# Three double slots in every gate/up chunk but the first, and each double slot's own remainder ahead of its weight sums

## What is computed

```python
D_MODEL, SEQ, D_FF = 2048, 256, 5632

def swiglu(h, wg, wu, wd):
    return (jax.nn.silu(h @ wg) * (h @ wu)) @ wd
...
x = x + 0.5 * swiglu(rmsnorm(x, ffn1_norm[i]), ffn1_wg[i], ffn1_wu[i], ffn1_wd[i])
x = x + hybrid_mixer(rmsnorm(x, mix_norm[i]), ...)
x = x + 0.5 * swiglu(rmsnorm(x, ffn2_norm[i]), ffn2_wg[i], ffn2_wu[i], ffn2_wd[i])
```

## Time and profile before

| | |
|---|---|
| median of 3 runs | 1819.16 us (1819.10 to 1820.21) |
| the profiled execution | 1821.51 us, its span 1819.7 us |
| TensorE matmuls busy | 1806.8 us, 99%, 8151 instructions |
| TensorE weight loads busy | 1486.1 us, 82% |
| VectorE busy | 1529.6 us, 84% |
| ScalarE busy | 1021.6 us, 56% |
| GpSimd busy | 247.9 us, 14% |
| granted TensorE clock | 0.999 of full speed, mean |
| DMA | 367.12 MB, mean 202 GB/s |

### The profile page before, as it was taken

One profiled execution on the slowest core, in us unless ns is written; L12 is line 12 of the kernel. 1 busy time (PEld: TensorE's weight loads), 2 busy tenths in 40 slices (PEclk: granted clock), 3 DMA queues, 4 the chain that ended last, 5 costly groups with the idle time before them and its releaser, 6 DMA issues.

```text
span 1819.7 us, 22566 instructions
## 1 busy us (share of the span) xinstructions
PE 1806.8 (99%) x8151; PEld 1486.1 (82%) x8152; DVE 1529.6 (84%) x1821; ACT 1021.6 (56%) x1320; POOL 247.9 (14%) x442
## 2 busy tenths in 40 slices
PE   9999999999999999999999999999999999999998
PEld 6888888888888888888788888888888888888886
DVE  7999898889888987678567867899888889988897
ACT  6555555455555555556577745555555455555554
POOL 2111111001111100000123300111111000221100
PEclk9999999999999999999999999999999999999999
DMA  7676766667767667766543655767767666777764
GB/s 242 210 218 205 218 205 216 194 200 211 227 199 216 199 212 211 207 207 199 151 131 113 208 174 184 215 204 218 213 196 211 218 203 191 218 216 213 234 210 149
DMA packets 199276, 367.12 MB, mean 202 GB/s; under 512 B 19012, under 2 KB 23856, under 8 KB 199056
## 3 DMA queue, kind: packets, MB, share of 16 engines
q1 hardware_dynamic: 185008, 352.37, 63.3%
q0 software_dynamic: 11648, 12.02, 2.2%
q10 hardware_dynamic: 2528, 1.52, 0.3%
HBM read 350.11 MB, written 4.19 MB: 195 GB/s over the span
## 4 chain that ended last, share of the span: by engine, by line
PE 75%; DVE 14%; DMA 7%; issue 2%; ACT 1%; DVEq 0%; ACTq 0%
PE ps L765 19%; PE ps L767 19%; PE ps L766 19%; DMA raw<-in_ffn_wu_dram 5%; PE ps L783 5%; PE ps L784 5%; PE ps L785 5%; DVE w_lo L1820 5%; DVE wt L1882 2%; PE ps L832 2%; DVE wt_lo L1892 1%; DVE wt L1885 1%; DMA raw<-in_ffn_wd_dram 1%; DVE wt L1887 1%; DVE w_lo L1900 1%
## 5 line engine op out<-in xcount | busy, mean ns | idle before, releaser
L1304 ACT ACTIVATE w_hi<-raw 128x1024 fp32r<-128x1024 f32 x579 | 609.4, 1059 | 415.3 <-PE ps L767 253.1
L1820 DVE TENSOR_TENSOR w_lo<-raw,w_hi 128x1024 fp32r<-128x1024 f32 x579 | 700.7, 1227 | 88.3 <-ACT w_hi L1304 84.4
L765 PE MATMUL ps<-w_hi,hT_hi 128*128 128x512 f32 x1356 | 531.3, 392 | 0.6 <-DVE w_lo L1820 0.4
L767 PE MATMUL ps<-w_hi,hT_lo 128*128 128x512 f32 x1356 | 528.3, 390 | 0.0
L766 PE MATMUL ps<-w_lo,hT_hi 128*128 128x512 f32 x1356 | 528.0, 389 | 0.0
L706 POOL DMA_DIRECT2D gu_raw<-gu_sq x352 | 187.8, 542 | 1082.1 <-DVE gu_sq L2057 1010.1
L765 PEld LDWEIGHTS ps<-w_hi,hT_hi 128*128 128x128 f32 x1356 | 254.7, 188 | 54.1 <-DVE w_lo L1820 2.5
L767 PEld LDWEIGHTS ps<-w_hi,hT_lo 128*128 128x128 f32 x1356 | 254.5, 188 | 53.7
L766 PEld LDWEIGHTS ps<-w_lo,hT_hi 128*128 128x128 f32 x1356 | 254.7, 188 | 51.3
L1355 ACT ACTIVATE wt_hi<-wt 128x1024 fp32r<-128x1024 f32 x152 | 160.3, 1055 | 164.1 <-DVE wt L1882 164.1
L765 PE MATMUL ps<-w_hi,guT_hi 128*128 128x512 f32 x496 | 193.0, 389 | 0.0
(11 more groups left out here) (306 smaller groups left out, 2156.2 us busy)
## 6 DMA issues: line engine op xcount, KB each, us to landing
raw<-in_ffn_wu_dram SPq DMA_DIRECT2D x176, 512.0 KB, 4.8
raw<-in_ffn_wd_dram SPq DMA_DIRECT2D x176, 512.0 KB, 4.9
raw<-in_ffn_wg_dram SPq DMA_DIRECT2D x175, 512.0 KB, 4.5
raw<-in_w_in_dram SPq DMA_DIRECT2D x88, 512.0 KB, 3.8
raw<-in_w_out_dram SPq DMA_DIRECT2D x32, 512.0 KB, 4.4
gu_raw<-gu_sq POOLq DMA_DIRECT2D x352, 32.0 KB, 3.7
x_parked<-x SPq DMA_DIRECT2D x8, 256.0 KB, 5.3
raw<-in_cmp_k_w_dram SPq DMA_DIRECT2D x8, 256.0 KB, 3.2
```

The lines of the kernel that those rows point to most:

```text
L765: mm(o, x_hi, w_hi[:, s, kk, :], start=begin, stop=False, skip_group_check=skip)
L767: ins = mm(o, x_lo, w_hi[:, s, kk, :], start=False, stop=last and kk == GK - 1, skip_group_check=skip)
L1304: act.activation(w_hi[:, c % SLOTS, :, :], raw[:, c % SLOTS, :, :], ACT.Copy).then_inc(hi_ready, 1)
L1820: tt(w_lo[:, s, :, :], raw[:, s, :, :], w_hi[:, s, :, :].bitcast(F32), ALU.subtract).then_inc(lo_ready, 1)
```

## The change

All gate/up chunks but the first take the table with three double slots, so 7 chunks of each FFN get one more (14 in all). The gate additions, the Silus and the sums for up of every chunk move to steps 0 and 1 of what follows. ScalarE's `gu_operand` and `gs_high` go to steps 9 and 11, VectorE's `gu_sums` to step 10 and its `gu_operand` to step 14 (9 in chunks 5, 6 and 10, which have no sums to make for the chunk before). In every double slot, those of the first chunk and of the down jobs too, VectorE makes the slot's own remainder first and the sums behind it. Since the sums now read a raw tile whose remainder is already done, SyncE waits for `t_ready` too before it loads such a buffer again. The core of the diff:

```diff
-CHUNK = [(GATE, 0), (GATE, 1), (GATE, 4), (GATE, 5), (GATE, 6), (PAIR, 2), (PAIR2, 2), (GATE, 7),
-         (UP, 0), (UP, 1), (PAIR, 3), (PAIR2, 3), (UP, 4), (UP, 5), (UP, 6), (UP, 7)]
...
+CHUNK = [(GATE, 0), (GATE, 4), (GATE, 5), (GATE, 6), (PAIR, 1), (PAIR2, 1), (GATE, 7), (UP, 0),
+         (PAIR, 2), (PAIR2, 2), (UP, 4), (UP, 5), (PAIR, 3), (PAIR2, 3), (UP, 6), (UP, 7)]
+NO_SUMS = (5, 6, 10)
...
-PAIRS = 2
+PAIRS = 3
...
-TURN_STEPS = [0, 1, 2, 3, 7]
+TURN_STEPS = [0, 1, 2, 3, 14]
...
                 if c >= SLOTS:
-                    sp.wait_ge(lo_ready, count(c - SLOTS + 1, i, per))
+                    sp.wait_ge(lo_ready, c - SLOTS + 1)
+                for f in range(2):
+                    if c - SLOTS - FFN0[f] in PAIR_SLOTS:
+                        sp.wait_ge(t_ready, pair_no(f, c - SLOTS) + 1)
...
                     for p, (kind, _) in enumerate(chunk_table(n)):
                         slot(f, c + p, kind, i)
-                        if n - 1 in LATE and n != PART0[1] and p < NT:
-                            late_silu(f, n - 1, p)
                         if n != PART0[1]:
-                            if p == gu_at:
+                            if p < NT:
+                                late_silu(f, n - 1, p, i)
+                            if p == 9:
                                 gu_operand(f, n - 1, i)
-                            if p == gu_at + 1:
+                            if p == 11:
                                 gs_high(n - 1, quad_no(f, n - 1), i)
...
-                        if p == 14 and n not in LATE:
-                            product1_copy(f, n, c + chunk_pairs(n)[-1], i)
-                        if p == 15 and n not in LATE:
-                            silu(f, n, i)
...
                     lo(c, i, CHUNK_SLOTS)
                     if kind == PAIR:
+                        weight_sums(f, c, i)
                         wt_low(f, c, 0, i)
-                if next_kind == PAIR:
-                    weight_sums(f, c + 1, i)
...
+                    low_at = 9 if n in NO_SUMS else 14
...
-                            if n - 1 in LATE and p == 0:
-                                gate_products(f, n - 1)
-                            if n - 1 in LATE and p == 1:
-                                right_sums(f, n - 1)
+                            if p == 0:
+                                gate_products(f, n - 1, i)
+                            if p == 1:
+                                right_sums(f, n - 1, i)
...
-                            if p == gu_at:
+                            if p == 10:
                                 gu_sums(f, n - 1, quad_no(f, n - 1), i)
-                            if p == gu_at + 1:
+                            if p == low_at:
                                 gu_operand(f, n - 1, quad_no(f, n - 1), i)
-                        if p == 14 and n not in LATE:
-                            gate_products(f, n, i)
-                            right_sums(f, n, i)
```

More of the change, by code:

```diff
@@ L596, in _, with load @@
         def _(sp):
-            def load(c, src, i=None, per=0, halves=None):
+            def load(c, src, halves=None):
                 if c >= SLOTS:
-                    sp.wait_ge(lo_ready, count(c - SLOTS + 1, i, per))
+                    sp.wait_ge(lo_ready, c - SLOTS + 1)
+                for f in range(2):
+                    if c - SLOTS - FFN0[f] in PAIR_SLOTS:
+                        sp.wait_ge(t_ready, pair_no(f, c - SLOTS) + 1)
                 s = c % SLOTS
@@ L1397, in silu, with late_silu @@
                                    scale=rs[:, RS_FFN2 if f else RS_FFN1, t:t + 1]).then_inc(silu_done, 1)
-            def late_silu(f, n, t):
+            def late_silu(f, n, t, i=None):
                 if t == 0:
-                    product1_copy(f, n, FFN0[f] + chunk_slot(n) + chunk_pairs(n)[-1])
-                silu(f, n, tiles=(t,))
+                    product1_copy(f, n, FFN0[f] + chunk_slot(n) + chunk_pairs(n)[-1], i)
+                silu(f, n, i, tiles=(t,))
             def gu_operand(f, n, i=None):
@@ L1473, in down @@
                         slot(f, c + g, kind)
-                        if n_last in LATE and g < NT:
+                        if g < NT:
                             late_silu(f, n_last, g)
@@ L1893, in wt_low, with slot @@
                    ALU.subtract).then_inc(t_lo_ready, 1)
-            def slot(f, c, kind, next_kind, i=None):
+            def slot(f, c, kind, i=None):
                 if kind == PAIR2:
@@ L2094, in ffn @@
                         continue
-                    slot(f, c + p, kind, None)
+                    slot(f, c + p, kind)
                     for g in after.get(p, ()):
                         g()
-                    if p + 1 < len(FIRST) and FIRST[p + 1][0] == PAIR:
-                        weight_sums(f, c + p + 1)
                 def chunk(n, i=None):
                     c = FFN0[f] + chunk_slot(n)
[L2103 to L2106, removed]
+                    low_at = 9 if n in NO_SUMS else 14
+                    for p, (kind, _) in enumerate(chunk_table(n)):
+                        slot(f, c + p, kind, i)
                         if n == PART0[1]:
@@ L2135, in down @@
                     for g, (h, p, kind, _) in enumerate(order):
-                        slot(f, c + g, kind, order[g + 1][2] if g + 1 < len(order) else None)
-                        if n_last in LATE and g == 0:
+                        slot(f, c + g, kind)
+                        if g == 0:
                             gate_products(f, n_last)
-                        if n_last in LATE and g == 1:
+                        if g == 1:
                             right_sums(f, n_last)
```

7 lines of the change are left out of this document (1 added, 6 removed).

## The result

| | before | after |
|---|---|---|
| median, 5 runs each on one chip | 1819.16 us (1818.53 to 1820.59) | 1839.04 us (1838.17 to 1839.14) |
| profiled execution, its span | 1821.51, 1819.7 us | 1838.17, 1836.4 us |
| the 14 changed chunks | 589.1 us | 610.9 us |
| chunks 1, 6, 7 of both FFNs | 254.3 us | 250.5 us |

The change makes the kernel slower: ratio 1.0105 [1.0094, 1.0116]. The prediction was 1830 in a range of 1812 to 1843, slower with 0.76.

A forecast was written before the change was run, and what follows sets the result against it. VectorE's round was to replace TensorE as the pace: 14 changed chunks at 43.3 us, less a 2.0 credit, +15.1; chunks 1, 6, 7 -4.6; down jobs nothing; net +10.5 on 1819.2, rounded to 1830 us, range 1812 to 1843.

The forecast's parts named there:

- VectorE's busy time, 41.74 us a round: Changed chunk: VectorE's 37.41 us in chunk 4 plus 4.33 for one more double slot, against TensorE's 41.48.
- Waits of 1.5 us a round: VectorE's idle time in a changed chunk, 0.5 + 0.4 + 0.6 us, making its round 43.3 us.
- Step 9: VectorE's sums at a double slot wait for this step's raw tile: 0.5 us idle, bounds 0 and 0.8.
- Step 12: VectorE waits for w_hi while ScalarE's gs_hi, ahead of it, waits for gu_sums: 0.6 us idle.
- Step 10: VectorE waits for w_hi, as ScalarE rounds guT_hi first: 0.4 us idle.
- The credit of 2.0 us for chunks 2 and 8: Total taken off the changed chunks' time because these two begin with a lead.
- Where TensorE waits: Per changed chunk: about 1.5 us at its start for Silu, 0.3 at the first double slot; some 25 in all.
- Chunks 1, 6, 7: Chunks after work with spare VectorE time: put at 41.9, 41.9 and 41.6 us, together -4.6 over both FFNs.
- Copies late (1842): Rival: late gu_raw copies delay w_hi of step 10, 0.9 us a round, +12.6 more; chance 0.15.
- TensorE sets the time (1810): Rival: a VectorE lead absorbs the waits, rounds of 41.48 to 41.74 us, -9.3 in all; chance 0.14.
- balance (1818): Rival: VectorE waits of 0.5 us, rounds of 42.3, +3.1 - 4.6, no difference; chance 0.10.
- The reorder does nothing: Rival: at double slots wt_lo comes 4.87 us after VectorE's start in either order; earlier remainder helps 0.2 us at most.

The follow-up runs named there:

- experiment 5: Changed kernel plus two unread VectorE reductions of 0.60 us each per chunk, at the sums for up, behind the gate additions: 1858.59 us, ratio 1.0222.
- experiment 7: Changed kernel with its new order and places, but before's tables (two double slots in most chunks, three in 5, 6, 10): 1821.82 us, ratio 1.0015.
- experiment 3: Changed kernel with ScalarE's guT_hi and gs_hi one step later, at steps 10 and 12: 1824.05 us, ratio 1.003.
- experiment 10: experiment 7 with later places for guT_hi, gs_hi, gu_sums and the remainders, as in the kernel before; gate additions stay late: 1816.11 us, ratio 0.9985.
- experiment 6: Kernel before plus two unread VectorE reductions of 0.60 us each per chunk, at the sums for up: 1833.07 us, ratio 1.0074.
- experiments 2: Changed kernel with the sums ahead of the slot's own remainder again, so third double slots without the new order: 1854.03 us, ratio 1.0192.
- experiment 8: experiment 3 with the four gu_sums made on GpSimd in place of VectorE: 1823.28 us, ratio 1.0027.

## Why the prediction was right, and where it was off

- **As a whole.** The direction and the mechanism held: VectorE's round is the pace, and TensorE stands mostly where the walk put it. The rounds of 43.64 us lie in the forecast's 42.8 to 43.8, but 1839.0 is 2 us above its own range of 1823 to 1837.
- **VectorE's busy time, 41.74 us a round.** Measured 41.72 in chunk 3 and 583.9 / 14 = 41.71 over the changed chunks. That VectorE's round, and not TensorE's 41.48, sets the pace: shown by experiment 5.
- **Waits of 1.5 us a round.** The marked ones come to 18.3 / 14 = 1.31. Step 9: 7.6 us in all, 0.54 a round (I said 0.5). Step 12: 0.62 in each of the ten chunks that make `gs` (I said 0.6); chunks 5 and 10 have none, where I had charged it to all 14, so it is 0.44 a round. Step 10: 0.17 in nine of these ten, and 1.40 in chunk 9 of the first FFN with its late copies, 0.2 a round (I said 0.4). Step 8: 0.16 to 0.38 in five chunks, where I had none.
- **What the sum lacked.** 43.64 - 41.71 - 1.31 = 0.62 us a round lie in unmarked gaps: 0.04 to 0.14 us between instructions of VectorE that wait for one another, as from 162.01 to 162.11 above. My 41.74 was a union of busy time and left them out, while they are path where the engine never rests. This is the term that was mis-sized: mean round 43.64 for 43.3, some 4.7 us over 14 rounds.
- **The credit of 2.0 us for chunks 2 and 8.** It failed. They took 44.16 and 44.51 in the first FFN, 43.39 and 42.91 in the second. Chunk 1 (42.27 for 41.48 of TensorE) ended with no lead left. In the first FFN both also waited longest for the raw tile of step 9, 0.98 and 1.17 us.
- **Where TensorE waits.** The excess over 0.2267 us a matmul, slot by slot, sums to 30.1 us: 19.5 at the chunks' starts, 1.4 a round (I said 1.5), 5.5 at the first double slot, 0.4 a round (I said 0.3), and 5.1 in the second and third, where I had none. "Some 25 us" was low by the same amount as the rounds.
- **Chunks 1, 6, 7.** I put them at 2 x 125.4 = 250.8 us; measured 250.5. The -4.6 became -3.8 because I had taken the first FFN's lengths of before for both, and the second's were shorter (254.3 in all, not 255.5). **The down jobs at nothing:** -0.45.
- **Copies late (1842).** In the changed kernel it happened once, in chunk 9 of the first FFN, the slowest round (45.09):

```profile
550.49 1.06 ACT L1411 ACTIVATE guT_hi<-gu_raw 128x1024 f32 x1 [1.12 <-DMA gu_raw<-gu_sq]
```

  The margin of 1 us that I gave it was about right: in the other changed chunks the last copy landed 0.7 to 1.6 us before `guT_hi` began. Late copies decided only in experiment 7.
- **TensorE sets the time (1810), balance (1818).** Out. They needed waits under 0.4 and of 0.5 us; experiment 3, with 0.7 a round left, has rounds of 42.6.
- **The reorder does nothing.** Wrong: 3 us in the old tables, 15 in the new. What I credited to it (1.14 us of filled wait) was the right mechanism, and I gave it too small a place among the rivals.
- **1830 against 1839.** Of the 9 us, 6.7 lie in the changed chunks (4.7 in the rounds, 2.0 in the credit) and 3.2 in the distance of the two profiled executions from their medians; chunks 1, 6 and 7 add 0.8, and chunk 0 and the down jobs take 1.2 back. That makes 9.5, and 19.9 - 10.5 = 9.4 were to be explained.

## What to carry over

When an engine has no spare time left, sum its start-to-start times, not its busy time, and count every wait of the round: 1.07 of 1.20 us that experiment 5 added came out. In the same kernel with some spare time (experiment 10) far longer waits cost nothing. Then look first at the engine that is *not* busy: two of ScalarE's steps, each one place too early, were 15 of the 20 us. Look at the granted clock of a window that is too long before all of it is put down to a wait. Give more work only to those rounds that follow a round with room, and fix an order before filling the room that it makes.

## What the runs showed of the hardware

- GpSimd's additions and VectorE's slow each other. Four of 128x128 took 1.30, 0.91, 1.45 and 1.32 us on GpSimd, where VectorE needs 0.28 to 0.29 each, and took 1.05 us from VectorE. Work of that kind moved to the idle engine bought nothing.
- TensorE's granted clock fell to half (1.2 of 2.4 GHz) for 3.41 us in chunk 1 of both FFNs in experiment 6 and in chunk 9 of the first FFN in experiments 2 and 7 (in experiment 6 also once before chunk 1 of the first FFN, at 7.3 us). The matmuls in these four chunks follow each other every 427 ns in place of 227, which makes 1.6 to 1.7 us each time. Right before, TensorE had stood for 1.84, 1.98, 2.23 and 2.07 us. That the stand brought the fall is not tested by a run. In the changed kernel the clock is full through all chunks, so it has no part in the loss.
- GpSimd begins two of its 22 sets of 16 copies 3.1 us later than the others, and the profile names nothing that it waits for (`issue`). In the changed kernel, in chunks 4 and 9:

```profile
195.65 8.50 POOL L706 DMA_DIRECT2D gu_raw<-gu_sq  x16 [34.75 <-DVE gu_sq L2051]
...
538.34 8.50 POOL L706 DMA_DIRECT2D gu_raw<-gu_sq  x16 [39.00 <-issue]
```

  That is 9.46 us from the start of chunk 4, and 12.68 from that of chunk 9. It is the same two sets in all twelve kernels: the 9th and the 17th begin 3.7 us after the transpose has ended, the others 0.6 to 0.7. Between lie 8 sets, 128 copies. The 17th falls into the down job behind chunk 5 of the second FFN, which has room. It is the same in experiment 8, where GpSimd's loop is written out, so the loop is not the cause. In the changed kernel the late 9th set made the slowest round, and it is behind the longest wait of experiment 7, 7.26 us against 1.4 to 4.6 elsewhere. What it is stays open.
